# ScalarE in the last step of the odd attention: the copies of two turned maps stand between the exponentials of the step's two maps

## The chip, the cores and the metric

One core of one Trainium2 chip runs the kernel. The metric is device time in microseconds from the start to the end of one launch. TensorE does the matmuls, VectorE and ScalarE the elementwise work and the copies out of PSUM, GpSimd a few masks, and SyncE issues the transfers of the weights. Each engine has its own instruction queue and runs it in order; the engines meet through semaphores.

## What is computed

Two networks of two layers each run one after the other on 256 tokens of width 1024. The first has an "even" layer and an "odd" layer; the change lies in the odd layer's attention: 16 query heads of 64 channels over 4 key heads, within 128 positions on either side, with a distance penalty (slope) and a learnt sink for each head. The result is multiplied by a gate and goes through the output weights.

```python
def odd_mixer(h, w_in, w_out, sink):
    proj = h @ w_in
    q, k, v, g = jnp.split(proj, [...], axis=-1)
    ...
    m, l, acc = banded_attention(q, k, v, slopes, 1, C_HALF_WINDOW)   # s = q k - slope * distance, masked; p = exp(s - m)
    M = jnp.maximum(m, sk)
    e = jnp.exp(m - M)
    y = acc * e[..., None] / (l * e + jnp.exp(sk - M))[..., None]
    ...
    return (y * jax.nn.silu(g)) @ w_out
```

## The kernel before

**Maps.** Each head's 256 by 256 probabilities are a map. The odd attention has 16 maps, 0 to 15 here, taken in pairs, and two maps of a pair fill one chunk (128 channels) of the output `y`. A step k of the attention handles pair k (maps 2k and 2k + 1) in its scores and exponentials, pair k - 1 in its turning and pair k - 2 in its product with the values. There are 8 pairs, so the steps run from 0 to 9, and step 7 is the last one that has exponentials: those of maps 14 and 15.

**What a map goes through.** TensorE writes the scores into a PSUM bank `sc`. VectorE adds the penalty table and takes the row's extremum (L605), then meets the sink (L611). ScalarE takes the exponential with its row sum, in two halves of 128 rows (L557), and the sink's exponential (L562). VectorE sums the denominator (L620), takes the reciprocal (L627) and scales the two halves (L636). TensorE turns the map (transposes, L512) into a PSUM bank `tp`. ScalarE copies the turned map to `probsT` (L572, called the turned copy below). TensorE multiplies `probsT` with the values into `yv`. VectorE multiplies `yv` by the gate into `yT` (L2778). The output weights want `yT` as a rounded high part (ScalarE, L520) and the rest (VectorE, L524).

**Weights.** They come in slots of 1 MB. A slot with split weights becomes a high part `w_split` on ScalarE (L777) and a low part `ring_rounded` on VectorE (L786), and TensorE forms three products: high weights with high data, high weights with low data, low weights with high data (`pe_split`, L690). Slots are put into the steps of the attention by a table (`FILL`, `AHEAD`). Step 6 has the last gate slot `odd9`, step 7 the modulation slots `ada1_10` and `ada1_11`, whose results VectorE reduces at L1980 in step 8. The low part of the first output slot `odd_out0` is made right behind these (`AHEAD["odd"][7]`); its high part was made two slots earlier.

**Order around step 7.** No scheduler moves anything: every engine's queue stands as the loops write it.

- TensorE (`pe_attention`, L463): in step 7 the scores of maps 14 and 15, the product of maps 10 and 11 with the values, the turning of maps 12 and 13, the slots `ada1_10` and `ada1_11`. In step 8 the product of maps 12 and 13 with the values, which waits for both turned copies (`pt_ready`); then the first three of eight chunks of `odd_out0`: high-high and high-low, the turning of maps 14 and 15, a wait for the low weights, and low-high. In step 9 the product of maps 14 and 15 with the values, and then the five other chunks of `odd_out0`.
- VectorE (`dve_attention`, L588): in step 7 L605 and L611 for maps 14 and 15, then L620 to L636 for map 14 and, behind a wait for its exponentials, for map 15, then `yT` of one chunk (L2778) and L524. In step 8 L1980 four times, L786 for `odd_out0`, L2778 and L524 again.
- ScalarE (`act_attention`, L542): in step 7 the exponentials of maps 14 and 15, the turned copies of maps 12 and 13, and L520 for a chunk. In step 8 the turned copies of maps 14 and 15 and L520.

The function that the change touches, and who calls it:

Of the kernel before, what the change touches and what calls it, by code (L numbers as in the profile page):

```python
# [314 lines left out]
def build(nc, x_d, w_d, vec_d, con_d, bias_d, lev_d, aux_d, row_d, out_d):  # L315
    ctx = ExitStack()
    with ctx:
# [34 lines left out]
        probsT = sb("probsT", [P, 2, 2, SEQ])  # L352
# [6 lines left out]
        tp = [ctx.enter_context(nc.psum_tensor(f"tp{i}", [P, 512], F32)) for i in range(2)]  # L359
# [15 lines left out]
        flat = lambda ap: ap.rearrange("p c t -> p (c t)")  # L375
# [11 lines left out]
        trans_done, pt_ready, pv_done, y_out = map(sem, ("trans_done", "pt_ready", "pv_done", "y_out"))  # L387
# [72 lines left out]
        turned_size = lambda m: 3 * P if causal(m) else 4 * P  # L460
# [58 lines left out]
        def act_y_high(act, chunk):  # L519
            act.post(nc.scalar.copy(y_high[:, chunk], yT[:, chunk]), s["y_high"])  # L520
# [6 lines left out]
        def act_normalise(act, m):  # L527

            act.take(s["token_scale"])
            if m["diff"] == 2:  # L530
                return
            if m["g"]:
                act.eng.wait_ge(probs_done, m["g"])
            for it in range(NT):
                pr = probs[:, m["g"] % 4, it, 0:sources(m, it)]
                ins = nc.scalar.activation(pr, pr, ACT.Copy, scale=stat[:, m["g"] % 4, 6 + it:7 + it])
                if it == 0:
                    act.do(ins)
            ins.then_inc(probs_done, 1)
            act.eng.wait_ge(probs_done, m["g"] + 1)  # L540

        def act_attention(act, phase, between=None, behind=None):  # L542

            ms = in_phase(phase)
            n = len(ms) // 2
            for k in range(n + 2):
                fill(act, act_slot, phase, k - 1)
                if between:
                    between(k)
                for m in ms[2 * k:2 * k + 2]:  # L550
                    st = stat[:, m["g"] % 4]
                    act.eng.wait_ge(biased, m["g"] + 1)
                    if m["slope"] is not None:
                        act_bias(act, m["b"] + BIAS_RING)
                    for it in range(NT):
                        pr = probs[:, m["g"] % 4, it, 0:sources(m, it)]
                        ins = nc.scalar.activation(pr, pr, ACT.Exp,  # L557
                                                   bias=st[:, it:it + 1], scale=-1.0, accum_out=st[:, 2 + it:3 + it])
                        if it == 0 or m["sink"] is not None:
                            act.do(ins)  # L560
                    if m["sink"] is not None:
                        ins = nc.scalar.activation(st[:, 4:6], st[:, 0:2], ACT.Exp, bias=V("sink", m["sink"]))  # L562
                    ins.then_inc(exp_done, 1)
                    act.eng.wait_ge(exp_done, m["g"] + 1)
                for m in ms[2 * k - 2:2 * k] if k else ():
                    if not m["trans"]:
                        continue
                    act.eng.wait_ge(trans_done, m["t"] + 1)
                    if m["t"] >= 2:
                        act.eng.wait_ge(pv_done, m["t"] - 1)  # L570
                    size = turned_size(m)
                    nc.scalar.copy(flat(probsT[:, m["t"] % 2])[:, 0:size], tp[m["t"] % 2][:, 0:size]).then_inc(pt_ready, 1)  # L572
                    act.eng.wait_ge(pt_ready, m["t"] + 1)
                for m in ms[2 * k:2 * k + 2] if phase == "even" else ():
                    act_normalise(act, m)
                if phase in NEEDED and 3 <= k < 3 + len(placed(phase)):
                    m = placed(phase)[k - 3]
                    act.eng.wait_ge(y_out, m["u"] + 1)
                    act_y_high(act, m["chunk"])
            if behind:  # L580
                behind()
            fill(act, act_slot, phase, n + 1)
            if phase in NEEDED and n + 2 < 3 + len(placed(phase)):
                m = placed(phase)[-1]
                act.eng.wait_ge(y_out, m["u"] + 1)
                act_y_high(act, m["chunk"])

        def dve_attention(dve, phase, finish, lam=None, between=None, behind=None):  # L588

# [67 lines left out]
        def act_bias(act, b):  # L657

            if b < N_BIAS:
                act.eng.dma_start(bias[:, b % BIAS_RING], bias_d[b]).then_inc(bias_landed[b % BIAS_RING], 16)  # L660
# [1729 lines left out]
        pair = lambda ap, i: flat(ap[:, 2 * i:2 * i + 2])  # L2390
# [11 lines left out]
        for l in range(2):  # L2402
            t = f"L{l}"
# [53 lines left out]
        def fill(e, use, phase, k):  # L2457

            key = phase if phase in FILL else phase[:-1]
            prefix = "" if phase in FILL else f"L{phase[-1]}"  # L2460
            for n in FILL[key].get(k, ()):
                use(e, prefix + n)
            if use is dve_slot:
                dve_ahead(e, phase, k)
# [98 lines left out]
        def _(eng):  # L2563
# [41 lines left out]
            def act_diff_last():  # L2605
                act_diff_square(B_HEADS - 1)
                act_sums_copy(act)

            act_attention(act, "even", lambda k: act_diff_square(k - 7) if k >= 7 else None,
                          act_diff_last)  # L2610
            act_highs(act, IDX["even_out1"])
# [14 lines left out]
            for n in ODD_FIRST:  # L2626
                act_slot(act, n)
            act_attention(act, "odd")
            for i in range(KC // 2):
                act_highs(act, IDX["odd_out1"] if i == 0 else min(IDX[f"odd_out{i}"] + 1, IDX["odd_out3"]))  # L2630
# [10 lines left out]
            for layer in range(2):  # L2641
                t = f"L{layer}"
                act_first_slots(act, layer)
                act_stick(act, layer)
                act_attention(act, f"moba{layer}", lambda k: act_decay_log(act, k))
                act_hgrn(act, layer)
                act_rwkv(act, layer)
# [323 lines left out]
```

## Time and profile before

| | us |
|---|---|
| median of three runs | 1266.6 (1266.57 to 1267.89) |
| the profiled execution, its own time | 1266.85 |
| its span from the first to the last instruction | 1265.0 |
| TensorE busy | 1240.2 (98%) |
| VectorE busy | 821.0 (65%) |
| ScalarE busy | 695.9 (55%) |
| GpSimd busy | 99.1 (8%) |

Busy time is time in which the engine executes, and it is no measure of how hard it is used: matmuls are pipelined and their ends are modelled. The chain that ended last, followed back from the end, is 91% TensorE. The odd attention's step 7 and 8 lie between 268 and 281 us of the span.

### The profile page before, as it was taken

The page shows a single profiled execution, that of the slowest core. Times are in us where ns is not written, and L with a number is a line of the kernel's source. Part 1 is how long each engine was busy: PE and PEld are TensorE (multiplying, and loading weights), DVE is VectorE, ACT ScalarE, POOL GpSimd, SP SyncE. Part 2 cuts the span into 40 slices and gives each one's busy share as a digit, 9 for nine tenths or more (in the row PEclk, how much of TensorE's full clock was granted, in tenths as well). Part 3 has the DMA queues.
Part 4 walks back from the last instruction along what each step waited for, and adds up shares of the span by engine and source line. Part 5 has one row for each costly group of instructions (what it writes and reads, how often), then busy time and mean ns, then how long its engine had stood idle before and what let it go on. Part 6 is the DMA issues. An engine that isn't in the chain of part 4 may idle for free.

```text
span 1265.0 us, 24522 instructions
## 1 busy us (share of the span) xinstructions
PE 1240.2 (98%) x10360; PEld 1122.1 (89%) x10360; DVE 821.0 (65%) x1219; ACT 695.9 (55%) x910; POOL 99.1 (8%) x83
## 2 busy tenths in 40 slices
PE   6999999999999999999999999999999999999998
PEld 6998999879999999899888888999999999888886
DVE  5455767886866879766655545766868857555533
ACT  4468546865856667245544435756567345544433
POOL 0000000000000330230000000000430130000000
PEclk9999999999999999999999999999999999999999
DMA  9867765725434433225555554544443335555552
GB/s 383 317 244 275 262 230 201 251 90 167 166 135 167 167 134 134 70 101 186 181 182 184 194 180 169 173 151 166 151 151 101 102 101 183 178 188 190 176 169 97
DMA packets 35102, 222.92 MB, mean 176 GB/s; under 512 B 3888, under 2 KB 8240, under 8 KB 9264
## 3 DMA queue, kind: packets, MB, share of 16 engines
q1 hardware_dynamic: 31104, 215.97, 48.7%
q10 hardware_dynamic: 3888, 5.38, 1.3%
q8 instruction: 82, 1.34, 0.4%
q14 instruction: 28, 0.23, 0.1%
HBM read 220.28 MB, written 1.05 MB: 175 GB/s over the span
## 4 chain that ended last, share of the span: by engine, by line
PE 91%; DVE 3%; ACT 2%; DMA 2%; issue 1%; POOL 0%; ACTq 0%; SPq 0%; DVEq 0%
PE pj L668 61%; PE yv L668 14%; PE sc L668 10%; PE tp L668 4%; DVE ring_rounded L786 1%; DMA big<-weights 1%; PE tp L512 1%; PE tp L2091 1%; DVE att_area L605 0%; DMA xT<-x_t 0%; ACT att_area L557 0%; ACT w_split L777 0%; ACT probsT L1757 0%; DVE scr_rounded L2824 0%; DVE xT L1115 0%
## 5 line engine op out<-in xcount | busy, mean ns | idle before, releaser
L786 DVE TENSOR_TENSOR ring_rounded<-ring,w_split 128x2048 fp32r<-128x2048 f32 x105 | 245.9, 2348 | 61.8 <-ACT w_split L777 58.5
L2328 DVE TENSOR_TENSOR ring_rounded<-ring,big_rounded 128x2048 fp32r<-128x2048 f32 x66 | 151.3, 2293 | 107.4 <-ACT big_rounded L2204 107.3
L777 ACT CAST w_split<-ring 128x2048 fp32r<-128x2048 f32 x105 | 200.3, 1908 | 29.4 <-PE pj L668 20.3
L668 PE MATMUL pj<-h_split,w_split 128*128 128x256 f32 x1264 | 172.7, 286 | 0.9 <-DVE h_split L2717 0.9
L668 PE MATMUL pj<-h_split,ring_rounded 128*128 128x256 f32 x1264 | 165.7, 281 | 0.7 <-DVE ring_rounded L786 0.7
L668 PEld LDWEIGHTS pj<-h_split,w_split 128*128 128x128 f32 x1264 | 156.5, 189 | 7.1 <-issue 5.9
L668 PEld LDWEIGHTS pj<-h_split,ring_rounded 128*128 128x128 f32 x1264 | 156.0, 188 | 2.3 <-issue 1.1
L2204 ACT CAST big_rounded<-ring 128x2048 fp32r<-128x2048 f32 x66 | 126.2, 1912 | 49.9 <-PE pj L668 48.3
L668 PE MATMUL pj<-hT_rounded,w_split 128*128 128x256 f32 x1136 | 147.0, 281 | 0.0
L668 PEld LDWEIGHTS pj<-hT_rounded,w_split 128*128 128x128 f32 x1136 | 139.7, 188 | 0.3 <-DVE hT_rounded L2722 0.2
L668 PE MATMUL sc<-big_rounded 128*128 128x512 f32 x176 | 67.8, 391 | 0.0
L668 PE MATMUL pj<-big_rounded 128*128 128x512 f32 x176 | 67.5, 389 | 0.0
L2428 ACT ACTIVATE big<-pj 128x512 f32<-128x512 f32 x32 | 19.1, 598 | 67.5 <-PE pj L668 67.5
L2213 ACT CAST big_rounded<-tp 128x512 fp32r<-128x512 f32 x22 | 12.9, 586 | 69.1 <-PE tp L2091 69.1
L557 ACT ACTIVATE att_area<-att_area,stat 128x256 f32<-128x256 f32 (+1 forms) x80 | 39.9, 499 | 17.8 <-DVE stat L605 7.5
L668 PE MATMUL yv<-big_rounded,yT_rounded 128*128 128x512 f32 x192 | 49.1, 398 | 0.1
L668 PE MATMUL yv<-big_rounded,rw_rounded 128*128 128x512 f32 x192 | 47.7, 390 | 0.0
L668 PE MATMUL yv<-ring_rounded,yT_rounded 128*128 128x512 f32 x192 | 47.5, 389 | 0.0
L1513 POOL TENSOR_TENSOR big<-big 128x512 f32<-128x512 f32 x16 | 30.7, 1918 | 200.3 <-DVE big L1429 190.0
L668 PEld LDWEIGHTS yv<-ring_rounded,yT_rounded 128*128 128x128 f32 x192 | 36.0, 188 | 7.5
L668 PEld LDWEIGHTS yv<-big_rounded,rw_rounded 128*128 128x128 f32 x192 | 35.9, 188 | 7.4
L668 PEld LDWEIGHTS yv<-big_rounded,yT_rounded 128*128 128x128 f32 x192 | 35.0, 188 | 8.1 <-issue 0.8
(396 smaller groups left out, 2132.3 us busy)
## 6 DMA issues: line engine op xcount, KB each, us to landing
ring<-weights SPq DMA_DIRECT2D x178, 1024.0 KB, 4.9
big<-weights SPq DMA_DIRECT2D x22, 1024.0 KB, 8.4
first_block<-biases ACTq DMA_DIRECT2D x26, 192.0 KB, 4.7
first_block<-biases SPq DMA_DIRECT2D x6, 192.0 KB, 8.6
xT<-x_t SPq DMA_DIRECT2D x1, 1024.0 KB, 5.1
con<-constants SPq DMA_DIRECT2D x1, 897.0 KB, 6.7
aux<-small SPq DMA_DIRECT2D x1, 832.0 KB, 10.5
out_t<-scr SPq DMA_DIRECT2D x3, 256.0 KB, 2.4
```

The source lines that it names most:

```text
L512: last = nc.tensor.transpose(tp[m["t"] % 2][:, at:at + P], probs[:, m["g"] % 4, it, jt * P:(jt + 1) * P], C("ident"))
L557: ins = nc.scalar.activation(pr, pr, ACT.Exp, bias=st[:, it:it + 1], scale=-1.0, accum_out=st[:, 2 + it:3 + it])
L668: return nc.tensor.matmul(out, lhsT, rhs, start=start, stop=stop, skip_group_check=True)
L777: act.post(nc.scalar.copy(high_home(w), ring[:, in_ring(idx)]), s["w_high"])
L786: dve.post(nc.vector.tensor_tensor(ring_r[:, at], ring[:, at], high_home(w).bitcast(F32), ALU.subtract), s["w_low"])
L1513: pool.tell(nc.gpsimd.tensor_tensor(d, b, b[:, :, n - 1:n].to_broadcast([P, 512 // (2 * n), 2 * n]), ALU.subtract), s["hgrn_diff"])
L2091: last = nc.tensor.transpose(tp[j % 2][:, (2 * c + T) * P:(2 * c + T + 1) * P], by_token(j, T)[:, c * P:(c + 1) * P], C("ident"))
L2204: act.tell(nc.scalar.copy(w_high(i), ring[:, in_ring(w_at(t, i))]), s["ffn_high"])
L2213: act.tell(nc.scalar.copy(hidden_high(j), tp[j % 2][:, :]), s["ffn_placed"])
L2328: dve.tell(nc.vector.tensor_tensor(w_low(t, i), w, value(w_high(i)), ALU.subtract), s["ffn_low"])
L2428: free(act, nc.scalar.activation(GATES[name], b[:, :], ACT.Tanh, scale=0.5), name)
```

## The change

The turned copies become a function, `act_turned`. In the odd attention's step 7, and there alone, it is called before the second map of the step instead of behind both. The other steps, the even attention, and the attention of the second network call it where the copies stood. Line numbers below the function move by 8.

```diff
                 if between:
                     between(k)
+                copies_between = phase == "odd" and k == n - 1
                 for m in ms[2 * k:2 * k + 2]:
+                    if copies_between and m is ms[2 * k + 1]:
+                        act_turned(act, ms[2 * k - 2:2 * k])
                     st = stat[:, m["g"] % 4]
                     act.eng.wait_ge(biased, m["g"] + 1)
...
                     ins.then_inc(exp_done, 1)
                     act.eng.wait_ge(exp_done, m["g"] + 1)
-                for m in ms[2 * k - 2:2 * k] if k else ():
-                    if not m["trans"]:
-                        continue
-                    act.eng.wait_ge(trans_done, m["t"] + 1)
-                    if m["t"] >= 2:
-                        act.eng.wait_ge(pv_done, m["t"] - 1)
-                    size = turned_size(m)
-                    nc.scalar.copy(flat(probsT[:, m["t"] % 2])[:, 0:size], tp[m["t"] % 2][:, 0:size]).then_inc(pt_ready, 1)
-                    act.eng.wait_ge(pt_ready, m["t"] + 1)
+                if k and not copies_between:
+                    act_turned(act, ms[2 * k - 2:2 * k])
...
+        def act_turned(act, pair):
+
+            for m in pair:
+                if not m["trans"]:
+                    continue
+                act.eng.wait_ge(trans_done, m["t"] + 1)
+                if m["t"] >= 2:
+                    act.eng.wait_ge(pv_done, m["t"] - 1)
+                size = turned_size(m)
+                nc.scalar.copy(flat(probsT[:, m["t"] % 2])[:, 0:size], tp[m["t"] % 2][:, 0:size]).then_inc(pt_ready, 1)
+                act.eng.wait_ge(pt_ready, m["t"] + 1)
```

ScalarE's queue of the kernel before, in the odd attention: the last gate slot, then step 7 with the exponentials of maps 14 and 15 (L557, L562), the turned copies of maps 12 and 13 (L572) and a chunk's high part (L520), then step 8's turned copies.

```order
L1959 ACTIVATE big<-pj 128x512
L557 ACTIVATE att_area,stat<-att_area,stat 128x256 x2
L562 ACTIVATE stat<-stat,vec 128x2
L557 ACTIVATE att_area,stat<-att_area,stat 128x256 x2
L562 ACTIVATE stat<-stat,vec 128x2
L572 COPY probsT<-tp 128x512 x2
L520 CAST big_rounded<-yT 128x256
L572 COPY probsT<-tp 128x512 x2
```

The same place in the changed kernel, where L560 and L565 are the exponentials, L593 the turned copies and L1967 the gate slot:

```order
L1967 ACTIVATE big<-pj 128x512
L560 ACTIVATE att_area,stat<-att_area,stat 128x256 x2
L565 ACTIVATE stat<-stat,vec 128x2
L593 COPY probsT<-tp 128x512 x2
L560 ACTIVATE att_area,stat<-att_area,stat 128x256 x2
L565 ACTIVATE stat<-stat,vec 128x2
L520 CAST big_rounded<-yT 128x256
L593 COPY probsT<-tp 128x512 x2
```

Two copies moved ahead of the three instructions of map 15's exponentials; everything ahead of and behind these rows stands as before.

VectorE's queue of the changed kernel, from map 15's normalising (L628 to L644, which waits for map 15's exponentials) to the low part of `odd_out0` (L794); the reductions at L1988, of which the first pair of rows stands here, lie between. The kernel before has the same rows under its own line numbers (L620 to L636, L2778, L1980, L786).

```order
L628 TENSOR_TENSOR stat<-stat 128x2
L635 RECIPROCAL stat<-stat 128x2
L644 TENSOR_SCALAR att_area<-att_area,stat 128x256 x2
L2786 TENSOR_TENSOR yT<-yv,big 128x256
L524 TENSOR_TENSOR yT_rounded<-yT,big_rounded 128x256
L1988 ISA diag,mod_raw<-pj,con 128x32
L1988 ISA mod_raw 128x1
```

Nothing moved on VectorE, nor on TensorE, GpSimd and SyncE.

## Rows read from the trace of the kernel before

**Rows 1.** Chain that ended last, 262 to 282 us: start, us, what.

```profile
262.38 5.72 PE pj L668 x48
...
270.73 0.61 ACT att_area L557 x2
...
272.33 0.61 ACT att_area L557 x2
...
273.59 0.30 ACT stat L562
...
273.99 0.17 DVE stat L620
...
276.90 2.30 DVE ring_rounded L786
...
279.25 0.98 PE pj L668 x6
...
281.24 9.54 PE pj L668 x78
```

**Rows 2.** Whom TensorE waited for, whole run: total us, times, longest us.

```profile
PE tp L668 <- DVE scr L818: 9.1, 1, 9.1
PE yv L668 <- ACT probsT L572: 2.3, 2, 2.1
PE yv L668 <- DMA big<-weights: 1.8, 2, 1.6
PE pj L668 <- DVE ring_rounded L786: 1.4, 4, 0.5
```

**Rows 3.** ScalarE in order of time, step 7: start, us, instruction.

```profile
272.00 0.30 ACT L562 ACTIVATE stat<-stat,vec 128x2 f32<-128x2 f32 x1
...
273.92 1.20 ACT L572 COPY probsT<-tp 128x512 f32<-128x512 f32 x2
275.15 0.41 ACT L520 CAST big_rounded<-yT 128x256 fp32r<-128x256 f32 x1
```

**Rows 4.** TensorE in order of time, steps 7 and 8 [idle before <-releaser].

```profile
270.09 1.09 PE L512 MATMUL tp<-con,att_area 128*128 128x128 f32 x8
271.12 1.95 PE L668 MATMUL pj<-big,cs 128*32 128x128 f32 x64
275.18 1.08 PE L668 MATMUL yv<-probsT,big 128*64 128x256 f32 x8 [2.11 <-ACT probsT L572]
276.19 0.97 PE L668 MATMUL pj<-big_rounded,w_split 128*128 128x256 f32 x6
...
277.71 1.03 PE L512 MATMUL tp<-con,att_area 128*128 128x128 f32 x8
279.25 0.98 PE L668 MATMUL pj<-big_rounded,ring_rounded 128*128 128x256 f32 x6 [0.50 <-DVE ring_rounded L786]
```

**Rows 5.** VectorE in order of time, steps 7 and 8.

```profile
273.99 0.16 DVE L620 TENSOR_TENSOR stat<-stat 128x2 f32<-128x2 f32 x1 [0.45 <-ACT stat L562]
...
274.39 0.74 DVE L636 TENSOR_SCALAR att_area<-att_area,stat 128x256 f32<-128x256 f32 x2
...
276.90 2.29 DVE L786 TENSOR_TENSOR ring_rounded<-ring,w_split 128x2048 fp32r<-128x2048 f32 x1
```

**Rows 6.** Whom TensorE waited for from 285 us to the end.

```profile
PE tp L668 <- ACT probsT L1757: 1.2, 8, 0.2
PE yv L668 <- issue: 0.9, 1, 0.9
```

**Rows 7.** By stretch: busy us of PE, PEld, DVE, ACT, POOL (instructions), granted clock, DMA.

```profile
271.00:275.20 4.20, 2.09 (x68) 1.71 (x66) 2.87 (x14) 3.94 (x13) 0.00 (x0) 1.00 0.32 133
...
1259.00:1261.00 2.00, 0.23 (x2) 0.00 (x0) 1.72 (x5) 0.98 (x3) 0.00 (x0) 1.00 0.67 251
1261.00:1263.00 2.00, 0.00 (x0) 0.00 (x0) 0.49 (x2) 0.72 (x1) 0.00 (x0) 1.00 0.35 129
1263.00:1264.00 1.00, 0.00 (x0) 0.00 (x0) 0.00 (x0) 0.00 (x0) 0.00 (x0) 0.69 0.78 289
```

## Prediction

> **What bounds the kernel now.** I read three views in this order: whom TensorE waits for in the whole run, the chain that ended last around steps 7 and 8, and the engines there in order of time.
>
> The first view alone suggests a gain. The longest single wait of TensorE after the 9.1 us at the start is for a turned copy, 2.11 us [rows 2, 4]: it is done with `ada1_10` and `ada1_11` at 273.07 (271.12 + 1.95) and starts the product of maps 12 and 13 with the values at 275.18, because ScalarE makes their turned copies last in the step, from 273.92 on [rows 3, 4]. The change makes them earlier.
>
> The chain does not pass through that wait. It leaves TensorE at the end of `odd9` (268.10, 262.38 + 5.72), passes through the exponentials of map 14 (270.73) and of map 15 (272.33 to 273.88), then through VectorE's normalising of map 15 (273.99) and what is queued behind it, up to the low weights of `odd_out0` (L786, 276.90 to 279.20), and only there goes back to TensorE, at 279.25 [rows 1]. TensorE had run dry once more at that point, for 0.50 us, with VectorE's L786 as releaser [rows 4]. So two waits lie one behind the other on TensorE, and it is the second one that holds the path; between them lie some 3.6 us of TensorE's work that fit without touching the end. The turned copies stand behind the chain on ScalarE: they start when map 15's exponentials are done.
>
> **The change part by part.** It adds and removes no instruction; it moves two copies past three instructions of one queue.
>
> What the moved copies gain. Map 14's last ScalarE instruction starts at 272.00 and the next instruction at 272.33 [rows 1, 3]. The copies start there, since the turning of maps 12 and 13 is done by 271.18 (270.09 + 1.09) [rows 4], so nothing else holds them. In the profile TensorE starts 1.26 us behind the first copy's start (275.18 - 273.92) [rows 3, 4]. After: 272.33 + 1.26 = 273.59, which is 1.59 us sooner, and the wait there shrinks from 2.11 to 0.52 us.
>
> What the exponentials behind them lose. The two copies take 1.23 us from start to the next instruction's start (273.92 to 275.15; the busy time is 1.20) [rows 3]. Map 15's exponentials start at 272.33 + 1.23 = 273.56 and end at about 275.11. There is no cover for this: map 15's scores were ready when ScalarE came to it, as the instruction had no wait of its own [rows 1], and VectorE was already waiting for the result, 0.45 us [rows 5]. That wait grows to 0.45 + 1.23 = 1.68 us. Behind it on VectorE's queue stand map 15's normalising, a chunk of `yT` with its low part, the four reductions of the modulation slots and L786. Nothing among them waited for anything else, so L786 starts at 276.90 + 1.23 = 278.13 and TensorE gets the low weights at 279.25 + 1.23 = 280.48.
>
> What TensorE does with the gain. From 273.59 it keeps its distances [rows 4]: the high products at 273.59 + 1.01 = 274.60, the turning of maps 14 and 15 at 274.60 + 1.52 = 276.12 (map 15's normalising ends at 274.39 + 0.74 + 1.23 = 276.36 [rows 5], and its half of the eight transposes comes some 0.5 us behind map 14's, so this does not wait), done at 277.15. Then it waits for the low weights until 280.48, 3.33 us instead of 0.50. Together 0.52 + 3.33 = 3.85 us of waiting instead of 2.61: again 1.23 or 1.24 more.
>
> What is hidden: the turned copies of maps 14 and 15 come sooner with their transposes, but their user stands behind the low products, so that is worth nothing. The move touches no transfer: step 7 issues none on ScalarE, and SyncE's transfers follow TensorE's slots.
>
> Behind 280.48 everything is paced by TensorE: the low products and maps 14 and 15 with the values (279.25 to 281.24, 1.99 us), and 9.54 us of output products without a break [rows 1]. From 285 us to the end no single wait of TensorE exceeds 0.9 us, and none is for a transfer [rows 6], so there is nothing that would swallow a delay of 1.2 us.
>
> The sum against the profiled execution's own 1266.85 us: plus 1.23, bounds 1.20 (the copies' busy time) and 1.26 (with the hand-over to the next engine): 1268.08. The profiled execution is 0.25 above the median of 1266.6, so against the median it is **1267.8 us**, 0.1% longer.
>
> The Trainium skill, "Perfetto Trace Analysis", section "Optimization Strategy", says to find the gaps on the engine that matters, look up which semaphore each waits for, and make that dependency start sooner. Taken for the 2.11 us gap, this gives the change a gain of 1.59 us, a sum of 1265.26; the trace's chain disagrees, since the next gap takes the gain back.
>
> **The rivals.**
>
> *The gap is worth what it shows.* If the low weights were not what TensorE waits for next, the 1.59 us would reach the end: 1266.6 - 1.59 = 1265.0. For it: the releaser of the 2.11 us is the copy. Against it: the second wait of 0.50 us for L786 [rows 4], and the fact that L786 stands behind map 15 on VectorE's queue, which the change does not touch. It would have to be a mistaken releaser. Even so, 1.59 us is less than 0.2%.
>
> *The delay is swallowed.* The median stays at 1266.6. It needs a wait for something that does not follow TensorE, a transfer above all. TensorE waits for transfers only twice, 1.8 us in all, and not behind 285 us [rows 2, 6]. It decides from any free wait of 1.2 us; I see none.
>
> *The clock falls, the case on the slower side.* TensorE's pause grows from 0.50 to 3.33 us, and from the last product at 276.12 to the next at 280.48 only eight transposes run. The profile shows the granted clock at 1.00 through the 2.11 us wait, and a fall at the end of the run: the last matmul ends at 1259.23, the clock is 1.00 up to 1263 and 0.69 on average in the next microsecond [rows 7], on its way to half, the 1.2 GHz level; that is a pause of a little over 4 us. The new pause of 3.33 us is shorter, the stretch of 4.36 us without a product is not. If the clock falls, the products that follow take twice as long while it is low: 1.99 us more for the low products and maps 14 and 15 alone, and 1.99 + 9.54 = 11.5 us more if it lasts through all the output products of that piece [rows 1]. I take the first, the least that a fall could touch, as no row shows how long the clock would stay low: 1267.8 + 2.0 = 1269.8, and 1279.3 as the upper bound. It decides from the point at which a pause of TensorE lets the clock go. The Trainium skill, "TensorE: Matmul & The Clock Gate", section "HAM oscillation — how this bites in real kernels", describes the same mechanism: a wait between batches of matmuls lets the clock drop, and the next batch starts cold. No pause of this length is in the trace to settle it: between the 2.11 us and the 9.1 us at the very start there is none [rows 2].
>
> **How the numbers follow.** The forecast has 0.80, the fallen clock 0.11, the swallowed delay 0.06, the gap's gain 0.03. About 0.2%, 2.5 us, is what a measurement of this kernel can tell from no change; the three runs alone span 1.3 us. The forecast, the swallowed delay and the gap's gain all lie within it; the fallen clock lies at 3.2 us or more, beyond it. With a little for the scatter of the runs: faster 0.02, same 0.85, slower 0.13. The range: the forecast's 1267.8 with a scatter of 0.7 us either way is 1267.1 to 1268.5; down to 1266.6 it takes in the swallowed delay, and up to 1269.6 the scatter and a short fall of the clock.
>
> **What the changed profile would show.** Right: the first wait near 0.5 us, the second, for the low weights, near 3.3 us; VectorE idle some 1.7 us before map 15's L620 (now L628); map 15's exponentials 1.23 us behind where they were relative to map 14's, and TensorE's last products all 1.2 us later. Wrong: the low weights' start unmoved relative to the end of `odd9`, or a granted clock under 1.00 behind 280 us, or the span's growth not the same from 281 us to the end.

## The result: 2.2 us slower, and the granted clock fell

| | before | after |
|---|---|---|
| median, us (19 runs each) | 1267.26 | 1269.49 |
| lowest to highest | 1266.43 to 1268.07 | 1268.89 to 1270.98 |
| profiled execution, own time | 1266.85 | 1270.45 |
| its span | 1265.0 | 1268.7 |
| its mean granted clock | 0.999 | 0.996 |

The granted clock is the share of its full clock that TensorE was given: 1.00 is the 2.4 GHz level, 0.50 the 1.2 GHz level. The ratio of the times is 1.0019, with a 95% interval of 1.0012 to 1.0027 (1.5 to 3.4 us): the changed kernel is slower by some 2.2 us. The forecast was 1.2 us slower; the range of 1266.6 to 1269.6 holds the median, but the loss is nearly twice the one that was worked out, and it is clear of no change.

Whom TensorE waits for after the change, over the whole run (total us, times, longest us); L794 and L593 are L786 and L572 of [rows 2]:

```profile
PE pj L676 <- DVE ring_rounded L794: 4.0, 3, 3.3
...
PE yv L676 <- ACT probsT L593: 0.7, 2, 0.5
```

The two waits changed places as worked out: 2.11 us became 0.5 and 0.50 became 3.3 [rows 2, 4]. TensorE in order of time, steps 7 and 8, to be read beside [rows 4]:

```profile
271.11 1.95 PE L676 MATMUL pj<-big,cs 128*32 128x128 f32 x64
273.57 1.08 PE L676 MATMUL yv<-probsT,big 128*64 128x256 f32 x8 [0.51 <-ACT probsT L593]
274.59 0.98 PE L676 MATMUL pj<-big_rounded,w_split 128*128 128x256 f32 x6
...
276.12 1.03 PE L512 MATMUL tp<-con,att_area 128*128 128x128 f32 x8
280.47 1.65 PE L676 MATMUL pj<-big_rounded,ring_rounded 128*128 128x256 f32 x6 [3.31 <-DVE ring_rounded L794]
282.05 1.98 PE L676 MATMUL yv<-probsT,big 128*64 128x256 f32 x8
```

On ScalarE and VectorE the delay came as worked out too: map 15's exponentials start behind the copies, at 273.55 instead of 272.33, and VectorE waits 1.69 us for them instead of 0.45 [rows 1, 5]:

```profile
273.55 0.51 ACT L560 ACTIVATE att_area<-att_area,stat 128x256 f32<-128x256 f32 x1
275.21 0.16 DVE L628 TENSOR_TENSOR stat<-stat 128x2 f32<-128x2 f32 x1 [1.69 <-ACT stat L565]
```

Every start of TensorE up to 280.47 lies within 0.02 us of the prediction's. But the six low products now take 1.65 us, where they took 0.98, and the product with the values 1.98, where product steps of that kind took 1.08. The chain that ended last (start, us, what) goes through the same pieces as [rows 1]. The low weights take the 2.30 us that they took, and all that TensorE does behind them takes longer:

```profile
278.12 2.30 DVE ring_rounded L794
...
280.47 1.65 PE pj L676 x6
282.12 1.91 PE yv L676 x8
284.02 10.67 PE pj L676 x78
294.69 0.57 PE tp L676 x8
```

From the low weights to the end of the output products it is 14.22 us (280.47 to 294.69); before it was 11.53 (279.25 to 290.78, [rows 1]). The difference of 2.69 us is the clock. By stretch (length, busy us and instructions of PE, PEld, DVE, ACT, POOL, granted clock, DMA share, GB/s):

```profile
276.00:279.00 3.00, 1.15 (x11) 0.91 (x9) 2.79 (x12) 1.57 (x3) 0.00 (x0) 1.00 0.01 3
279.00:280.00 1.00, 0.00 (x0) 0.00 (x0) 1.00 (x1) 0.00 (x0) 0.00 (x0) 0.85 0.00 0
280.00:286.00 6.00, 5.53 (x23) 4.18 (x24) 3.04 (x8) 1.85 (x3) 1.18 (x3) 0.50 0.00 0
286.00:287.00 1.00, 1.00 (x9) 1.00 (x8) 0.31 (x3) 0.77 (x1) 0.31 (x1) 0.73 0.00 0
287.00:290.00 3.00, 3.00 (x28) 3.00 (x27) 2.96 (x3) 0.00 (x0) 0.00 (x0) 1.00 0.14 25
```

The clock fell in the pause, near 279.7, to 0.50, the 1.2 GHz level, and came back in the microsecond from 286 on. All 19 runs of the changed kernel have a mean clock of 0.996 to 0.998. Their times lie in two groups, 13 runs at 1268.89 to 1269.73 us and 6 at 1270.34 to 1270.98; the profiled execution is of the upper one, and none of the lower one was profiled. So the rival "the clock falls" came about beside the forecast's delay. But 1.23 + 2.69 = 3.92 us is more than the medians differ by, and the runs before scatter as well. What are the two terms worth in the median, and does the kernel before lose clock too?

### The profile page after: what moved, and what is told of

Read it like the earlier page. It is cut to its first block, busy times and chain, and to the rows that moved or that the text cites. A ratio compares the mean times of both kernels' runs of the same rounds, so it can differ in the third digit from the quotient of the medians.

```text
span 1268.7 us, 24522 instructions
## 1 busy us (share of the span) xinstructions
PE 1242.0 (98%) x10360; PEld 1122.3 (88%) x10360; DVE 821.2 (65%) x1219; ACT 695.9 (55%) x910; POOL 99.0 (8%) x83
## 4 chain that ended last, share of the span: by engine, by line
PE 90%; DVE 4%; ACT 3%; DMA 2%; issue 2%; POOL 0%; ACTq 0%; SPq 0%; DVEq 0%
PE pj L676 60%; PE yv L676 14%; PE sc L676 10%; PE tp L676 4%; DVE ring_rounded L794 2%; DMA big<-weights 1%; PE tp L512 1%; PE tp L2099 1%; ACT w_split L785 0%; DVE att_area L613 0%; DMA xT<-x_t 0%; ACT att_area L560 0%; ACT probsT L1765 0%; DVE scr_rounded L2832 0%; DVE xT L1123 0%
## 5 line engine op out<-in xcount | busy, mean ns | idle before, releaser
L794 DVE TENSOR_TENSOR ring_rounded<-ring,w_split 128x2048 fp32r<-128x2048 f32 x105 | 245.9, 2348 | 61.8 <-ACT w_split L785 58.2
L560 ACT ACTIVATE att_area<-att_area,stat 128x256 f32<-128x256 f32 (+1 forms) x80 | 39.9, 499 | 17.8 <-DVE stat L613 7.5
```

Of the source, the lines that this page charges most:

```text
L560: ins = nc.scalar.activation(pr, pr, ACT.Exp, bias=st[:, it:it + 1], scale=-1.0, accum_out=st[:, 2 + it:3 + it])
L794: dve.post(nc.vector.tensor_tensor(ring_r[:, at], ring[:, at], high_home(w).bitcast(F32), ALU.subtract), s["w_low"])
```

## Experiments

"Filled" below means that TensorE multiplies the identity matrix with ones into a free PSUM bank in one of its pauses. The result is read by nobody, and the dependencies between the engines stay as they were, save that the filled first wait also asks for semaphores that were reached before.

**The loss without the clock: a first filling, too long.** To the changed kernel:

```diff
-                pe_split(pe, "odd_out0", (y_high, yT_r), ks=range(3), between=turn)
+                pe_split(pe, "odd_out0", (y_high, yT_r), ks=range(3),
+                         between=lambda: (turn(), pe_turning(sc[0], 22)))
```

> The changed kernel, with 22 idle matmuls of 128 columns on TensorE behind the turning of maps 14 and 15, in the pause before the low weights; their output is read by nobody. Theory A (two prices: 1.23 us because the copies stand ahead of map 15's exponentials, and about 1 us in the median because the clock falls in the pause): the low weights still come 1.23 us later than before, the granted clock stays at 1.00, and the time is 1.0 to 1.4 us above the kernel before, that is about 1.0 us below the changed kernel's median. Theory B (the fall of the clock is only seen, and the 2.2 us come from the order on ScalarE and VectorE): about 2.2 us above the kernel before, as the changed kernel.

Measured: 1270.31 us, ratio 1.0023 (1.0014 to 1.0033). Both expectations miss. TensorE in order of time shows why:

```profile
276.99 5.08 PE L676 MATMUL sc<-con 128*128 128x128 f32 x44
281.82 0.95 PE L676 MATMUL pj<-big_rounded,ring_rounded 128*128 128x256 f32 x6
```

Each of these matmuls runs as two records of 0.11 us, so the filling takes 4.8 us, not 2.7, and itself holds the low products back, to 281.82 instead of 280.47. What it shows is the clock: the low products take 0.95 us again, and the mean clock of all nine runs is 0.999 or 1.0. It says nothing on the size of the loss.

**A second pause of middle length.** To the kernel before, ahead of L786:

```diff
+                if phase == "odd" and k == n:
+                    for _ in range(2):
+                        dve.do(nc.vector.tensor_copy(flat(vfirst), con[:, 0:2 * SEQ]))
```

> The kernel before, with two extra copies of 128x512 on VectorE ahead of the low part of odd_out0 (some 1.2 us, written to a buffer that is free there). TensorE waits as much in all as in the changed kernel, some 3.8 us, but in two pauses (2.1 and 1.7 us) with 2.6 us of products and transposes between them. Theory A, with the fall caused by one long pause: 1.1 to 1.4 us above the kernel before, granted clock 1.00. Theory C (the sum of the waiting decides, however it is split): the clock falls as in the changed kernel, 2.0 us or more above the kernel before.

Measured: 1267.68 us, ratio 1.0003 (0.9994 to 1.0012). The two copies take 0.93 us in the trace, not 1.2, and the low products start 0.9 us later than before in step 8. Neither theory expected no change in the median. The single runs tell more: four of the eleven have a clock of 0.999 or 1.0, and their median is 1267.78; the runs of the kernel before at that clock in the same comparison have 1266.86. That is 0.92, the copies' time. The seven runs at 0.997 or 0.998 have 1267.65, no more than the kernel before's own runs at that clock (1267.68). So the kernel before also has runs with a lower clock, and in those an extra 0.9 us ahead of the low weights costs nothing that the medians show.

**The kernel before, for the clock of its runs.** No edit.

> The kernel before itself, for the granted clock of each of its runs. Theory D (the clock falls in a part of its own runs, during or behind the 2.11 us wait): the runs are of two kinds, some with a mean clock of 0.999 near 1266.5 us, the others with 0.998 near 1267.4 us, and a fall costs about 0.9 us here, since the products and the turning then take some 1.4 us longer of which 0.50 us is hidden by the wait for the low weights. Theory A as first put (the clock never falls in the kernel before): a mean clock of 0.999 in all runs, and no tie between clock and time.

| mean clock of the run | runs | us |
|---|---|---|
| 0.999 or 1.0 | 4 | 1266.14 to 1266.42 |
| 0.997 or 0.998 | 7 | 1267.20 to 1268.27 |

No run of these eleven lies between. Of the 33 runs of the kernel before that were measured beside them, 11 have a clock of 0.999 or 1.0 (median 1266.71) and 22 a lower one (median 1267.63); one of the 22 is as fast as the first kind, 1266.32 at 0.998. The profiled execution is of the second kind, and shows where; TensorE in order of time, then by stretch, then the piece of its chain that [rows 1] have at 281.24:

```profile
271.41 1.95 PE L668 MATMUL pj<-big,cs 128*32 128x128 f32 x64
275.47 1.49 PE L668 MATMUL yv<-probsT,big 128*64 128x256 f32 x8 [2.11 <-ACT probsT L572]
276.89 1.65 PE L668 MATMUL pj<-big_rounded,w_split 128*128 128x256 f32 x6
...
279.55 1.03 PE L512 MATMUL tp<-con,att_area 128*128 128x128 f32 x8
280.34 0.95 PE L668 MATMUL pj<-big_rounded,ring_rounded 128*128 128x256 f32 x6
```

```profile
275.00:276.00 1.00, 0.53 (x6) 0.38 (x8) 0.90 (x4) 0.83 (x2) 0.00 (x0) 1.00 0.00 0
276.00:279.00 3.00, 3.00 (x16) 2.24 (x13) 2.86 (x10) 0.00 (x0) 0.00 (x0) 0.50 0.00 0
279.00:280.00 1.00, 1.00 (x9) 1.00 (x9) 0.97 (x3) 0.00 (x0) 0.00 (x0) 0.78 0.00 0
280.00:283.00 3.00, 2.85 (x24) 2.12 (x23) 0.67 (x2) 1.88 (x4) 0.00 (x0) 1.00 0.01 3
```

```profile
282.52 9.54 PE pj L668 x78
```

Behind the same 2.11 us wait the clock is at 0.50 from about 276.0 on, half a microsecond after TensorE went on. From the product with the values to the low products it takes 4.87 us (275.47 to 280.34) where it took 4.07 with the wait of 0.50 us in it (275.18 to 279.25, [rows 4]), and to the 78 output products 7.05 (275.47 to 282.52) instead of 6.06 (275.18 to 281.24, [rows 1, 4]), that is 0.99 more. The wait for the low weights is gone, since they were there before TensorE was. So the wait that looked free to remove is not free in two runs of three: it costs 0.9 us through the clock. The chain that ended last in this execution goes through the turned copies, not through the low weights.

The mean clock alone does not say where the clock fell. In the profiled execution of the next kernel it is 0.998 with a clock of 1.00 through both steps: the fall comes behind TensorE's last matmul, in a stretch like the one at the end of [rows 7]:

```profile
1261.00:1263.00 2.00, 0.00 (x0) 0.00 (x0) 0.44 (x1) 0.72 (x1) 0.00 (x0) 0.53 0.37 136
```

That a low mean clock in the kernel before stands for a fall behind the 2.11 us wait is shown by one trace of it, and for the other runs argued from the two levels of their times.

**The first wait of the kernel before, filled.**

```diff
+                    if around and k == len(ms) // 2:
+                        pe.eng.wait_ge(biased, ms[-1]["g"] + 1)
+                        pe_turning(sc[0], 9)
                     pe.eng.wait_ge(pt_ready, pair[-1]["t"] + 1)
```

> The kernel before, with 9 idle matmuls (two passes each, some 2.0 us) on TensorE in the 2.11 us wait for the turned copies of maps 12 and 13; nothing else moves. Theory D: the clock stays at 1.00, every run is near 1266.5 us, and the median is 0.5 to 1.0 us below that of the kernel before. Theory A as first put: no change, within 0.3 us.

Measured: 1266.05 us, against 1267.42 for the kernel before on the same chip; ratio 0.9992 (0.9983 to 1.0001), and nine of eleven runs at 0.999 or 1.0. With 18 idle records of 0.12 us on TensorE the clock stays up and the time is shorter, though the interval just reaches no change. A second time:

> The kernel before with its 2.11 us wait filled with 9 idle matmuls, once more, as the base for the two kernels measured beside it. Near 1266.1 us, mean clock 0.999 or 1.0 in nearly all runs.

Measured: 1266.29 us, against 1267.52; ratio 0.9994 (0.9985 to 1.0002), eleven of eleven runs at 0.999 or 1.0.

Both are also some 0.5 us below the full-clock runs of the kernel before (1266.7), which the clock cannot explain. The traces show where part of it lies. TensorE in the second network, the kernel before, then the busy time of TensorE alone (length, busy us and instructions, granted clock, DMA share, GB/s) in the kernel before and in this one:

```profile
516.98 0.27 PE L668 MATMUL yv<-scr,probsT 64*64 64x64 f32 x1 [0.92 <-issue]
```

```profile
510.00:523.00 13.00, 11.68 (x324) 1.00 0.27 86
510.00:523.00 13.00, 12.59 (x334) 1.00 0.25 86
```

Near 517 us TensorE stands idle for 0.92 us, and the profile shows nothing that it waits for. This idle time is 0.53 to 0.92 us in the six profiled executions without idle matmuls; with them it is 0.62 in one and gone in the six others. Why is not shown. It makes a filled kernel faster for a reason other than the clock, so the price of the clock behind the first wait is better read from the two kinds of runs, 0.92 us.

**The second wait of the changed kernel, filled to measure.** As the first experiment, with 13 in place of 22.

> The changed kernel with 13 idle matmuls (two passes each, some 2.9 us) behind the turning of maps 14 and 15, so that they end before the low weights come at about 280.5 us. Theory D: the clock stays at 1.00, and the kernel is 1.0 to 1.4 us slower than the kernel before with its own wait filled, that is 1267.5 to 1267.9 us, and 1.5 to 2.0 us faster than the changed kernel without the filling (1269.5 us). Theory B (the order on ScalarE and VectorE costs 2.2 us whatever the clock): near 1269.5 us.

Measured: 1267.94 us, 1.55 us below the changed kernel's median. TensorE in order of time: the filling ends before the low weights, and the products run at full clock.

```profile
277.95 3.07 PE L676 MATMUL sc<-con 128*128 128x128 f32 x26
281.42 0.97 PE L676 MATMUL pj<-big_rounded,ring_rounded 128*128 128x256 f32 x6 [0.41 <-DVE ring_rounded L794]
282.31 1.08 PE L676 MATMUL yv<-probsT,big 128*64 128x256 f32 x8
```

That puts the clock's part of the changed kernel at some 1.5 us in the median (1.0 to 2.4 when the runs are resampled). The idle time near 517 us is gone here too, so by this pair alone part of the 1.5 may not be the clock. Without any filling the same size comes out: the full-clock runs of the kernel before and the copies' 1.2 us make 1267.9, and the median is 1269.49. Against the kernel before at full clock (1266.7) the filled kernel leaves 1.2 us, the term of the forecast; against the filled kernel before it leaves 1.9. To see which holds, the pair was run again beside a kernel with one copy only between the exponentials:

```diff
                     if copies_between and m is ms[2 * k + 1]:
-                        act_turned(act, ms[2 * k - 2:2 * k])
+                        act_turned(act, ms[2 * k - 2:2 * k - 1])
...
-                if k and not copies_between:
+                if copies_between:
+                    act_turned(act, ms[2 * k - 1:2 * k])
+                elif k:
                     act_turned(act, ms[2 * k - 2:2 * k])
```

with 9 matmuls in the first wait and 3 in the second.

> Only the turned copy of map 12 between the exponentials of maps 14 and 15, that of map 13 behind both; the first wait of TensorE is filled with 9 idle matmuls, the second with 3. What is still open is whether the part of the loss that is left with a full clock is the copies' time ahead of map 15's exponentials (1.25 us by the traces) or more (the medians differ by 1.9 us). Theory E (the copies' time alone): one copy costs half, 0.6 us above the filled kernel before, and the low weights come 0.6 us later after the end of odd9 than there. Theory F (something else in the changed order costs about 0.6 us as well): 1.0 us or more above the filled kernel before.

> The changed kernel with its second wait filled with 13 idle matmuls, once more. Theory E: 1.1 to 1.4 us above the filled kernel before on the same chip. Theory F: 1.7 to 2.1 us above it.

| waits filled | median, us | start of the scores in step 7 to the low products, us |
|---|---|---|
| before | 1266.29 | 11.23 (268.24 to 279.47) |
| one copy between | 1267.53 | 11.86 (269.18 to 281.04) |
| two copies between | 1268.03 | 12.47 (268.18 to 280.65) |

In the trace each copy costs 0.61 to 0.63 us, as Theory E has it, and nothing else moved in the step. In the medians the first copy costs 1.24 and the second 0.50, and two cost 1.74. Pooled over both times the two filled kernels differ by 1.8 us, with a resampled 95% interval of 1.3 to 2.1. So Theory E is shown for the step. The medians are what was expected of Theory F: some 0.5 us of their difference lies outside the step, in places that the edit doesn't touch. Two such places show in the traces. In the profiled execution with one copy between, the clock fell at 33 us already (first row), and its mean clock is 0.998 for that reason. Near 996 us the first of the two executions of the filled changed kernel stands idle with nothing to wait for (second row), the second does not:

```profile
33.00:37.00 4.00, 3.78 (x40) 3.15 (x40) 1.55 (x12) 0.42 (x1) 0.00 (x0) 0.57 1.02 408
```

```profile
996.23 0.27 PE L676 MATMUL yv<-scr,probsT 64*64 64x64 f32 x1 [0.52 <-issue]
```

Idle time of that kind, 0.17 to 0.80 us near 996, is in five of the seven profiled executions with idle matmuls and in none of the six without. Whether it makes up the whole 0.5 us is open: the second execution, at 1267.30 us, is the fastest of its eleven runs.

**The low weights earlier.** On VectorE, L786 for `odd_out0` between map 14's normalising and map 15's, where VectorE waits anyway (0.45 us in the kernel before, 1.69 in the changed one, of the 2.3 us that L786 takes); once in the kernel before, once in the changed one, and once in the kernel before with its first wait filled:

```diff
                 dve_ahead(dve, phase, k - 1)
                 for m in ms[2 * k:2 * k + 2]:
+                    if phase == "odd" and k == n - 1 and m is ms[2 * k + 1]:
+                        dve_lows(dve, IDX["odd_out0"])
```

> The kernel before, with the low part of odd_out0 made on VectorE between the normalising of map 14 and that of map 15. Theory A: TensorE's second wait of 0.50 us goes, the first of 2.11 us stays, and the time is 0.3 to 0.6 us below the kernel before; against it the changed kernel with the same edit is 0.8 to 1.2 us faster. Theory B: no difference between this and the changed kernel with the same edit, or this one the faster.

> The kernel before with the low part of odd_out0 between the normalising of maps 14 and 15, and with the 2.11 us wait filled with 9 idle matmuls. Theory D: without the filling the fall of the clock ate the gain; with it the second wait is gone at full clock and the time is 0.3 to 0.7 us below the kernel before with its wait filled, near 1266.0 us. If the low weights were not what the second wait is for: no difference from the kernel before with its wait filled.

> The changed kernel, with the low part of odd_out0 made on VectorE between the normalising of map 14 and that of map 15, where VectorE waits for map 15's exponentials, and not behind both. Theory A: the low weights are there at about 275.9 us, TensorE's second wait is at most 0.5 us and is for map 15's normalising, the clock stays at 1.00, and the time is 1.0 to 1.7 us below the kernel before: now the first wait, which the change shortens by 1.59 us, is the one that counts. Theory B (the order of copies and exponentials costs on its own): at or above the kernel before.

| low weights ahead of map 15's normalising | median, us | ratio to before | runs at 0.999 or 1.0 |
|---|---|---|---|
| kernel before | 1267.64 | 0.9999 (0.9990 to 1.0008) | 3 of 11 (1266.01 to 1266.36) |
| kernel before, first wait filled | 1265.69 | 0.9990 (0.9981 to 0.9999) | 10 of 11 |
| changed kernel | 1264.89 | 0.9982 (0.9973 to 0.9991) | 10 of 11 |

In the kernel before the edit brings nothing in the median, where 0.3 to 0.6 us were expected. The single runs show why: the three at full clock have a median of 1266.32, 0.5 us below the full-clock runs of the unedited kernel (1266.86), and the eight others 1267.73, like its runs at a lower clock (1267.68), in which the second wait is gone anyway. With the first wait filled as well it is at 1265.69, 0.36 us below 1266.05, as expected, though the runs of the two overlap. In the changed kernel, with no filling, it is 2.6 us faster than the kernel before, more than the 1.0 to 1.7 expected, and 2.75 us faster than the kernel before with the same edit, where 0.8 to 1.2 were expected without a fall of the clock in that one. TensorE in order of time:

```profile
273.93 1.08 PE L678 MATMUL yv<-probsT,big 128*64 128x256 f32 x8 [0.52 <-ACT probsT L593]
274.94 0.98 PE L678 MATMUL pj<-big_rounded,w_split 128*128 128x256 f32 x6
...
277.31 0.66 PE L512 MATMUL tp<-con,att_area 128*128 128x128 f32 x4 [0.24 <-DVE att_area L646]
277.73 0.96 PE L678 MATMUL pj<-big_rounded,ring_rounded 128*128 128x256 f32 x6
278.69 1.08 PE L678 MATMUL yv<-probsT,big 128*64 128x256 f32 x8
```

No wait above 0.52 us is left in the two steps. Against the kernel before at full clock (1266.86 in this comparison) it is 2.0 us faster, of which 1.87 lie in the step (11.24 us from the start of the scores at 268.01 to the low products before, 9.37 here, 268.36 to 277.73), and another 0.6 us lies in the runs of the kernel before in which the clock falls. This is the fastest version of the study, and it needs the change: with the low weights made early and the clock up in both, it is 0.8 us below the kernel before with its first wait filled (1264.89 against 1265.69). The copies between the exponentials pay once the low weights no longer stand behind the delayed map.

## Why the prediction was right or wrong, point by point

- **Which wait holds the path.** Right for executions at full clock: the gain of 1.59 us at the first wait was taken back at the second (0.51 and 3.31 us, where 0.52 and 3.33 were worked out). In the executions of the kernel before in which the clock falls it is the first wait that holds the path. The rule of the Trainium skill, "Perfetto Trace Analysis", section "Optimization Strategy", that a gap's dependency be made to start sooner, would have given 1.59 us of gain; the changed kernel lost. It came true once the next gap was closed as well (1264.89 us).
- **The price of the copies.** Right: 1.23 us forecast, 1.22 in the changed trace (280.47 against 279.25 for the low products), 0.63 for one copy. The full-clock runs of the kernel with 0.92 us of extra copies on VectorE confirm that a delay of L786 reaches the end whole.
- **The clock, the step that failed.** The sum has no term for it, before or after the change. *Before:* the text said that the profile shows the clock at 1.00 through the 2.11 us wait and took this for the kernel. It was true of one execution. In two runs of three the clock falls behind that very wait, which costs 0.9 us. A sign was in the three times that were known: 1266.57, 1266.60 and 1267.89 look like the two levels, and I read them as scatter of 1.3 us. What it costs after the change is the next point.
- **The fall after the change.** It was named, with its place and mechanism, but held at 0.11 and left out of the sum. All 19 runs have a mean clock of 0.998 or less, and the fastest of them, 1268.89 us, is 1.0 us above what the copies alone make of the kernel before at full clock. The reason given, that the new pause of 3.33 us is shorter than the 4 us after which the clock fell at the end of the run, was no argument, since it falls behind 2.11 us in two runs of three. The mechanism that the Trainium skill describes ("TensorE: Matmul & The Clock Gate", section "HAM oscillation — how this bites in real kernels") is the one that the trace shows, products at the lower clock behind a wait. Its price was 2.69 us in the profiled execution and some 1.5 in the median, where 1.99 had been taken as the least. The time worked out for this rival, 1269.8, lies close to the measured 1269.49 in part by luck: its clock term is 0.5 too high and its base of 1266.6 is 0.7 too low.
- **The sum.** Full clock 1266.7, plus 1.2 for the copies, plus some 1.5 for the fall in the changed kernel, gives 1269.4; measured 1269.49. The 1.5 was taken from runs of the same kernel, so this closes the account and is no test of it; with the filled kernel before as the base, 0.5 us stay open. The median before is 1267.3, since falls are in it as well, and so the difference is 2.2 and not 2.7. The forecast had the copies' term alone, and no fall on either side. That its range holds the median is luck: the loss of 2.2 us has in it two falls that the sum has not, one on each side.

## What to carry to other kernels

When a change shifts a wait on TensorE from one place to another, its length is not its whole price: look at which executions have a lower granted clock, and compare the clocks of several runs with their times before a single profile is taken for the kernel. A wait whose removal seems to bring nothing because the next one takes it back should be removed together with the next one; here the pair brought 2.6 us where each alone brought nothing or a loss. A few idle matmuls in a pause are a cheap way to see what the clock does there; what they bring in the run's time is to be checked in the step itself, since idle time far from it differed here between the kernels with and without them.

## What the runs showed of the hardware that was not expected

The clock of one and the same program falls in some executions and not in others, behind a wait of 2.11 us: by the mean clock 7 of 11 runs, against 19 of 19 for the changed kernel, whose pause is 3.31 us. In the kernel before the fall came at about 276.0 us, after TensorE had gone on at 275.47; in the changed kernel near 279.7, within the pause. Why it comes in a given execution is not settled by these runs. The time at the lower clock differs as well: the changed kernel's profiled execution was at 0.50 through 280 to 286 us, that of the kernel before through 276 to 279 us.
